# Query-key products and seeds of even and odd heads over four array quadrants in an RWKV-7 recurrence

## The reference

```python
def step(state, inp):
    r_t, w_t, k_t, v_t, a_t, b_t = inp
    sa = jnp.einsum('bhij,bhj->bhi', state, a_t)
    state = state * w_t[:, :, None, :] + sa[..., None] * b_t[:, :, None, :] + v_t[..., None] * k_t[:, :, None, :]
    return state, jnp.einsum('bhij,bhj->bhi', state, r_t)
```

## Time and profile before

| | us |
|---|---|
| median of 3 runs | 3779.99 |
| the runs | 3774.95 to 3780.49 |
| the profiled execution | 3774.45 |
| its span | 3772.6 |
| TensorE busy, share of the span | 91% |
| VectorE, ScalarE, GpSimd busy | 47%, 28%, 30% |
| mean granted TensorE clock | 0.954 |
| recurrence of layer 1, layer 2 | 672.95 to about 866, 2526.13 to about 2719 |

### The profile page before, as it was taken

The page is one execution under the profiler, slowest core; times in us unless marked ns, Lnnn a source line. Parts: engine busy times, 40 slices in busy tenths (PEclk is TensorE's granted clock), DMA queues, the critical chain, the costliest instruction groups (busy, mean ns, idle before and its releaser), DMA issues.

```text
span 3772.6 us, 61018 instructions
## 1 busy us (share of the span) xinstructions
PE 3427.3 (91%) x23080; PEld 2462.0 (65%) x23080; DVE 1784.7 (47%) x3061; ACT 1068.7 (28%) x1875; POOL 1121.2 (30%) x940
## 2 busy tenths in 40 slices
PE   7889887898999999999988888779889999999997
PEld 3444444886667888888734445458765688888884
DVE  5689996344342222222348899844335122222224
ACT  3343224443122111122133432244412112122122
POOL 1274341651212222222114543335412222222221
PEclk9999998998999999999999998889999999999998
DMA  3100000000101111111111000000011111111111
GB/s 119 38 27 22 19 20 18 1 0 20 59 12 56 50 50 44 44 53 47 34 49 39 11 22 21 18 19 0 1 34 49 35 51 44 50 45 50 50 39 45
DMA packets 43864, 132.74 MB, mean 35 GB/s; under 512 B 9280, under 2 KB 11840, under 8 KB 43072
## 3 DMA queue, kind: packets, MB, share of 16 engines
q1 hardware_dynamic: 37280, 122.41, 10.0%
q10 hardware_dynamic: 6432, 8.40, 0.9%
HBM read 117.15 MB, written 5.24 MB: 32 GB/s over the span
## 4 chain that ended last, share of the span: by engine, by line
PE 59%; DVE 14%; DVEq 11%; issue 10%; ACT 2%; POOLq 2%; POOL 1%; ACTq 1%; DMA 0%; SPq 0%
PE bank L1021 14%; PE bank L1023 14%; PE bank L1022 14%; DVEq L1615 8%; DVE M L1611 8%; PE bank L751 3%; PE bank L629 2%; PE wide L601 2%; DVE PB L1627 2%; PE wide L751 1%; PE wide L606 1%; DVEq L1612 1%; DVE WK L1613 1%; PE bank L719 1%; POOLq L1503 1%
## 5 line engine op out<-in xcount | busy, mean ns | idle before, releaser
L1502 POOL TENSOR_TENSOR WL<-WR,WH 128x1024 fp32r<-128x1024 f32 x160 | 389.8, 2436 | 1492.0 <-ACT WH L1305 1491.3
L629 PE MATMUL bank<-X,WR 128*128 128x512 f32 x1088 | 532.2, 633 | 19.2 <-ACT A L1189 9.9
L1021 PE MATMUL bank<-XH,WH 128*128 128x512 f32 x1280 | 517.4, 404 | 19.8 <-DVE XL L1548 10.2
L1023 PE MATMUL bank<-XH,WL 128*128 128x512 f32 x1280 | 501.5, 392 | 0.0
L1022 PE MATMUL bank<-XL,WH 128*128 128x512 f32 x1280 | 501.5, 392 | 0.0
L1884 DVE TENSOR_TENSOR Y<-Y,bank 128x512 f32<-128x512 f32 x256 | 175.9, 687 | 492.1 <-PE bank L1023 492.1
L1021 PE MATMUL bank<-HH,WH 128*128 128x512 f32 x1024 | 400.4, 391 | 0.0
L1023 PE MATMUL bank<-HH,WL 128*128 128x512 f32 x1024 | 398.6, 389 | 0.0
L1022 PE MATMUL bank<-HL,WH 128*128 128x512 f32 x1024 | 398.4, 389 | 0.0
L629 PEld LDWEIGHTS bank<-X,WR 128*128 128x128 f32 x1088 | 206.0, 200 | 270.6 <-issue 243.8
L1305 ACT ACTIVATE WH<-WR 128x1024 fp32r<-128x1024 f32 x160 | 168.2, 1053 | 736.3 <-PE bank L1023 727.7
(11 more groups left out here) (275 smaller groups left out, 5141.7 us busy)
## 6 DMA issues: line engine op xcount, KB each, us to landing
WR<-in_w SPq DMA_DIRECT2D x128, 512.0 KB, 3.5
WR<-in_w_in SPq DMA_DIRECT2D x34, 512.0 KB, 3.5
WR<-in_w_out SPq DMA_DIRECT2D x16, 512.0 KB, 3.5
WR<-in_w_gate SPq DMA_DIRECT2D x16, 512.0 KB, 5.8
Y<-in_xT SPq DMA_DIRECT2D x2, 2048.0 KB, 13.1
out_T<-X SPq DMA_DIRECT2D x1, 4096.0 KB, 11.8
QZS<-QZ ACTq DMA_DIRECT2D x48, 64.0 KB, 2.0
QZS<-QZ ACTq DMA_DIRECT2D x64, 48.0 KB, 2.0
```

The source lines that it names most:

```text
L629: mm = e.matmul(BK_[hf], WR[:, i % RING, kt, :], X[:, kt, hs(hf)], start=kt == 0, stop=kt == KT - 1)
L1021: e.matmul(BK_[b], WH[:, s, w, :], high[:, kt, q], start=kt == 0, stop=False)
L1023: mm = e.matmul(BK_[b], WL[:, s, w, :], high[:, kt, q], start=False, stop=kt == kts - 1)
L1502: e.tensor_tensor(WL[:, s, :, :], WR[:, i % RING, :, :], WH[:, s, :, :].bitcast(F32), ALU.subtract)
```

## The change

On TensorE, products of even and odd heads are issued in one call, in the order (even, chunk 0), (odd, chunk 1), then (even, chunk 1), (odd, chunk 0), for each source and pair; so are the seeds. The call of the products for the next tile stands behind the last odd merge and ahead of `solved` (before: the even group ahead of that merge, the odd group between `solved` and `transitions`). The call of the seeds stands between `chain(T, 0)` and `from_state(T, 0)` (before: the even group there, the odd group at the tile's end). On VectorE both `mask_seeds` come behind the copy of the state of chunk 0 and ahead of that of chunk 1. Ahead of the loop TensorE issues all products, then all seeds; VectorE's order there is as before.

```diff
--- before.py
+++ after.py
@@ -704,34 +704,43 @@
             def was_read(T, bank, use):
                 e.wait_ge(rb[bank].free, rb[bank].read(T, use))
 
-            def products(T, g):
-
-                free(T, g, ("hE", "hO")[g])
+            def decayed(src, bank, col, h0, signals=False):
+
+                for turn in range(2):
+                    for g in range(2):
+                        c = g ^ turn
+                        mm = e.matmul(BK_[bank + g][chunk(c), col:col + 2 * CH], src[feats(g), h0 // 2, chunk(c)],
+                                      AR[feats(g), h0 // 2, :, chunk(c)], start=True, stop=True)
+                        if signals and turn:
+                            mm.then_inc(rb[bank + g].full, 1)
+
+            def products(T):
+
+                for g in range(2):
+                    free(T, g, ("hE", "hO")[g])
                 e.wait_ge(tilde_ready, T * N_TILDE + 4)
                 settle(e)
-                pair_products(BK_[g], 0, g)
-                pair_products(BK_[g], 4 * CH, g + 2).then_inc(rb[g].full, 1)
-
-            def pair_products(bank, col, h):
-
-                for j, src in enumerate((BT, KTL)):
-                    for c in range(2):
-                        mm = e.matmul(bank[chunk(c), col + 2 * CH * j:col + 2 * CH * (j + 1)],
-                                      src[feats(h), h // 2, chunk(c)], AR[feats(h), h // 2, :, chunk(c)],
-                                      start=True, stop=True)
-                return mm
-
-            def seed_products(T, g):
-
-                free(T, 2 + g, ("aE", "aO")[g])
+                decayed(BT, 0, 0, 0)
+                decayed(KTL, 0, 2 * CH, 0)
+                decayed(BT, 0, 4 * CH, 2)
+                decayed(KTL, 0, 6 * CH, 2, signals=True)
+
+            def seed_products(T):
+
+                for g in range(2):
+                    free(T, 2 + g, ("aE", "aO")[g])
                 settle(e)
-                pair_products(BK_[2 + g], 0, 4 + g)
+                decayed(BT, 2, 0, 4)
+                decayed(KTL, 2, 2 * CH, 4)
                 for j in range(3):
-                    for c in range(2):
-                        mm = e.matmul(BK_[2 + g][chunk(c), 4 * CH + CH * j:4 * CH + CH * (j + 1)],
-                                      AR[feats(g), j, 0, chunk(c)], BT[feats(g), j, chunk(c)],
-                                      start=True, stop=True)
-                mm.then_inc(rb[2 + g].full, 1)
+                    for turn in range(2):
+                        for g in range(2):
+                            c = g ^ turn
+                            mm = e.matmul(BK_[2 + g][chunk(c), 4 * CH + CH * j:4 * CH + CH * (j + 1)],
+                                          AR[feats(g), j, 0, chunk(c)], BT[feats(g), j, chunk(c)],
+                                          start=True, stop=True)
+                            if turn and j == 2:
+                                mm.then_inc(rb[2 + g].full, 1)
 
             def by_token(T):
 
@@ -888,24 +897,20 @@
                 merge_x(T, 1, LEVELS)
                 was_read(T, 4, f"UE{LEVELS - 1}")
                 merge_u(T, 0, LEVELS)
-                if more:
-                    products(T + 1, 0)
                 was_read(T, 5, f"UO{LEVELS - 1}")
                 merge_u(T, 1, LEVELS)
+                if more:
+                    products(T + 1)
                 solved(T, 0)
                 solved(T, 1)
-                if more:
-                    products(T + 1, 1)
                 transitions(T)
                 outputs(T)
                 chain(T, 0)
                 if more:
-                    seed_products(T + 1, 0)
+                    seed_products(T + 1)
                 from_state(T, 0)
                 from_state(T, 1)
                 chain(T, 1)
-                if more:
-                    seed_products(T + 1, 1)
 
             def head_sums(bank, squares, hf):
 
@@ -978,9 +983,8 @@
                             mm = e.matmul(BK_[2 * n + hf], PW[:, i, :], PZ[:, i, hs(hf)], start=True, stop=True)
                         mm.then_inc(b.full, 1)
                 meet(e, L, 1)
-                for g in range(2):
-                    products(L * NB, g)
-                    seed_products(L * NB, g)
+                products(L * NB)
+                seed_products(L * NB)
                 with e.Fori(0, NB - 1) as t:
                     rwkv_tile(L * NB + t, True)
                 rwkv_tile(L * NB + (NB - 1), False)
@@ -1709,8 +1713,9 @@
                 for c in range(2):
                     full(T, 6 + c, f"S{c}")
                     e.tensor_copy(ST8[:, 1 - c, :, :], heads3(6 + c, 3 * HD)).then_inc(rb[6 + c].free, 1)
-                    if more:
-                        mask_seeds(T + 1, c)
+                    if more and c == 0:
+                        mask_seeds(T + 1, 0)
+                        mask_seeds(T + 1, 1)
 
             with e.Fori(0, DEPTH) as L:
```

## The result

| | before | changed |
|---|---|---|
| median of 14 runs, us | 3778.14 | 3787.41 |
| the runs, us | 3774.51 to 3781.58 | 3782.29 to 3798.55 |
| span of the profiled execution, us | 3772.6 | 3785.2 |
| TensorE busy, us | 3427.3 | 3415.3 |
| mean granted TensorE clock | 0.954 | 0.954 |

The ratio is 1.0029, with a 95% interval of 1.0021 to 1.0038: the changed kernel is slower by 8 to 14 us, a little more than what can be told from no change. TensorE has 12 us less to do.

The account below looks back on a forecast made before the run. It took the chain of waits at the border between tiles, not TensorE's busy time, as the bound. 14 borders x 0.53 - 0.5 ahead of the loop = +6.9 us, on a median of 3779.99: 3786.9, range 3777 to 3797.

Parts of the forecast that it names:

- How fast four quadrants are: TensorE's products and seeds: a round costs the same with four quadrants; products take 0.88 us instead of 1.76.
- Step 1: Products moved between last odd merge and solved: they delay WU's last copy and the transitions, +0.27 us per tile.
- Step 3: VectorE's new order at the border: transposes wait for the later copy of state 1; +0.53 us per tile, Step 1 included.
- Step 2: Seeds of all groups ahead of from_state: nothing on the path; the odd seeds' 0.79 us behind the chain go.
- Step 4: Ahead of the loop: VectorE's mask of odd products no longer waits for TensorE, 2 x -0.24 = -0.5 us.
- The collision: Rival, border: VectorE's odd seed addition and GpSimd's addition shut each other out, +0.51 us; 3794.1, slower, 8%.
- The wait for copy 1: Rival: transposes' wait for the copy of state 1 doesn't bind, GpSimd's mask sets the border; 3777.3, 11%.
- The quadrants did overlap: Rival claimed the opposite: no overlap in this order, products cost 0.88 us more per tile; 3799.2, slower, 5%.
- All of TensorE's 1.7 us on the path: Rival: all the TensorE issue time saved shortens each tile, 14 x -1.67 = -23 us; 3756.6, faster, 8%.

Follow-up runs that it names:

- only_products: Kernel before with only the products moved and paired as changed; seeds and VectorE's order as before: 23.68 us a middle tile (before 23.33, changed 23.75), total 3783.45.
- tb_last: Changed kernel with the transposes that wait for the copy of state 1 put last on TensorE and ScalarE: 23.07 us a middle tile, total 3768.18.
- copy_between: Changed kernel with VectorE's copy of state 1 back between the two seed masks, TensorE as changed: 23.50 us a middle tile, total 3783.08.
- products_gap_busy: `products_gap` plus twelve useless transposes filling TensorE's wait for the copy of state 1: 22.82 or 22.83 us in all middle tiles, total 3771.10.
- old_prologue: Changed kernel with the order of before ahead of the loop only: first tiles 27.31 and 29.21 us, middle tiles 23.75 but for one, total 3789.88.
- gap_tb_last: Changed kernel with the edits of `products_gap` and `tb_last` together: 22.19 us a middle tile, median of 10 runs 3766.76 against 3778.25 before, ratio 0.9968.
- only_seeds: Kernel before with only the seeds and VectorE's order as changed: 23.38 to 23.40 us in five of twelve middle tiles, 23.46 to 25.22 in the others, total 3790.15.
- products_gap: Changed kernel with the products' call moved behind solved, ahead of the transitions: 22.82 us in two middle tiles, 23.56 to 24.63 in the other ten, total 3791.76.
- two_quadrants: Changed kernel with the even group issued ahead of the odd one, two quadrants at a time: 24.24 us a middle tile, total 3791.40.

## Why the prediction was right or wrong

**The number and the sign held, the class did not.** 3786.9 against 3787.41, inside the range of 3777 to 3797. The likeliest outcome was given as "no difference", at its slow edge, 0.49 against 0.43 for slower; by the prediction's own line of 0.2% the interval of 1.0021 to 1.0038 is slower. That the total came within 0.5 us is luck: the base was 1.85 too high and the difference 2.4 too small. In the profiled pair the parts were off in both directions too. Twelve middle borders were forecast to cost 6.4 and the middle tiles cost 5.5; the first tiles were forecast to cost 1.1 and cost 4.8; 3.3 more lie outside the recurrence, where the forecast had nothing. The mechanism of a middle tile is what the prediction had right.

**How fast four quadrants are: right.** Eight rounds of 0.11 forecast for the products, 0.90 us in all measured.

**Step 1, right in kind, sized too small.** Forecast +0.27, measured +0.37. The 0.10 lies in the step "starts at 783.60 and takes 0.35; then 0.88 of products": between the last merge's issue and the first product there is a gap of 0.12 (in the chain of waits the last twelve merges start at 793.23; with the 0.35 that the sum gave them they end at 793.58, and the first product starts at 793.70), which I had allowed for only in the upper bound, as sequencer steps. The products took 0.02 more than forecast, and the merge started 0.04 earlier behind XS. That taking the odd products out of their gap gives nothing was right: the transitions started 0.30 after WU's copy, as before. `only_products` shows the step by itself, 0.35 to 0.37.

**Step 3, right in kind, sized too large.** The copy of state 1 ended 7.32 us after the start of the transitions; the sum had 7.34 (794.50 less 787.16). But from its end to the first transposes it took 0.13, not 0.26: the further sequencer step of 0.11 that I had added does not show. Transposes to first merge: 1.13 for 1.18. That 0.05 is the 0.25 from the last transpose to the merge, which I had read in the earlier trace rows where the transposes start 0.21 apart, at half the clock. At full clock in the changed kernel it is 0.20 against the 0.11 between two transposes, so what a drain there could cost is 0.09 a tile and not 0.14. So step 1 and 3 together came to 0.42 per tile instead of 0.53. `tb_last` and `copy_between` show the wait by taking it away in two ways.

**Step 2, right.** The seeds' move costs nothing, and `copy_between` against `only_products` even gives 0.18 for it, close to the "0.16 earlier" in step 3.

**Step 4 and the first tiles were what failed.** The -0.24 per layer from the first product to the first merge was nearly right (8.83 to 8.65 and 8.88 to 8.66, so -0.18 and -0.22). But I left it at that and took the first tiles as middle ones. TensorE now idles 2.8 and 2.6 us ahead of the first merge and runs the first merges at half the clock. The first tiles took 4.8 us more where two borders' 1.1 stood in the sum. `products_gap_busy` ties what the fronts lost to the clock; `old_prologue` won back 2.5 us in one layer and lost 1.3 in the other. The waits that the profile calls "issue" in the first tile of layer 2 add up to 2.6 us before, 3.1 in the changed kernel and 4.7 in `old_prologue`, and no experiment took them apart; this stays open.

**The rivals.** The collision did not happen, by a hair: the odd addition took 0.36, starting 0.02 after GpSimd's had ended (803.60), where 0.05 was forecast. The wait for copy 1 did bind. The quadrants did overlap. "All of TensorE's 1.7 us on the path" was wrong in the changed kernel, but two thirds of it could be had: `gap_tb_last` is 1.14 a tile under before.

**What was in none of them** is a price for idling. The forecast read the granted clock of 1.00 in the earlier trace rows as given. It goes with a TensorE that waits 0.73 us at the border; with 1.35 the clock sometimes falls. In the changed kernel's profile that touched one middle tile (24.19), in `only_seeds` six, in `products_gap` ten. The changed kernel's fourteen runs spread over 16 us, those of before beside them over 7, but this is no sign of it: in another series the kernel before spread over 16.5 itself, and `gap_tb_last`, without a fall at a border, over 15.4.

## What to carry to other kernels

Faster matmuls pay only if what stands behind them isn't late: put a packed call into a gap where the engine waits anyway (0.9 us a tile here), and not ahead of the step that starts the next engine's work. When two steps of another engine are reordered to release one consumer earlier, look for the first instruction in a third queue that waits for the one moved back, and put the instructions that do not need it ahead of it (0.68 a tile). In a stage of small matmuls, look at what the waits do to TensorE's clock: an order that leaves it one longer wait can cost more than it saves (22.82 a tile became 23.56 to 24.63 in ten of twelve).

## What the runs showed of the hardware that was not expected

- Behind waits of 1.25 to 1.43 us between tiles TensorE came back at 1.2 GHz at 14 of 70 borders: three transposes there took up to 0.90 us in place of 0.49 to 0.54. Twelve transposes without use in that wait made the two recurrences 13.3 us shorter. With waits of 0.52 to 0.69 for the copy of state 1 (`tb_last`, `gap_tb_last`), or of 0.56 to 0.78 for the mask (before), there was no such fall.
- In `two_quadrants` TensorE does not hold a matmul back behind earlier ones that queue for another quadrant: eight start per 0.22 us as soon as the odd group is in the queue, and the first of solved starts at 765.56, ahead of products that stand before it in the queue and start up to 765.88.
- Four quadrants fed in turn by 128-column fp32 calls start eight instructions per 0.22 us, two quadrants four.
